# Recurrence of an encoder layer: the chunk inverse by products over 128 partitions, with full transposes of Z

## The chip, the cores and the metric

The kernel runs on one core of a Trainium2 chip. The metric is the device time of one execution in microseconds (us), the median of several runs; lower is better. The layer is computed for 2048 + 512 tokens (one stream of 2560 rows).

## The reference

One encoder layer: a combined projection, two mixers side by side (grouped attention, and RWKV-7 read in both directions), then a routed expert network with 16 experts. The changed part is the RWKV-7 recurrence:

```python
def wkv7_scan(r, decay, k, v, kk_neg, kk_b, reverse):
    def step(state, inp):
        r_t, w_t, k_t, v_t, an_t, b_t = inp
        sa = jnp.einsum('bhij,bhj->bhi', state, an_t)
        state = (state * w_t[:, :, None, :] + sa[..., None] * b_t[:, :, None, :]
                 + v_t[..., None] * k_t[:, :, None, :])
        return state, jnp.einsum('bhij,bhj->bhi', state, r_t)
```

It has 8 heads of 64 channels, each with a state of 64x64, and runs once forward and once backward. The kernel doesn't step token by token: it takes 64 tokens (a chunk) at a time. Inside a chunk the dependence of each token on those before it is a triangular 64x64 system per head, and the kernel inverts its matrix.

## The kernel before, in words

The program is a chain of stages, each a block of five instruction streams: attention inputs, attention, the inputs of the recurrence (`rwkv_inputs`), the recurrence (`recurrence`, L1194), output projection and routing, choice of tokens, experts. A stage starts when the one before it has ended.

**Layout.** Channels lie on partitions, two heads to a tile of 128 partitions (partitions 0 to 63 and 64 to 127, `halves`); four pairs (`RT` = 4, index `j`) make the 8 heads. The two directions are `g` = 0 and 1 and are independent; each has its own tiles and its own PSUM banks (`pX`, `pP`, `pZ`, `pS`). There are `NCH` = 40 chunks; direction 1 walks them backwards. A turn is the work on one chunk in both directions, half of it on chunk n (the state enters, the output leaves) and half on chunk n+1 (its inverse is prepared).

**Products.** All are plain fp32 matmuls of 64 contracted rows by 64 columns, one for each head (`heads`, L1470 to L1475). With `cross` set, the result of head h goes to the partitions of the other half. The PE program is unrolled over all 40 chunks; the programs of the other engines loop.

**The inverse.** `x3` gives the matrix, `x4` its transpose. Both are masked and get the identity (`begin`, L1404 to L1412), in `zy`: Z (index 0) and Y (index 1), kept side by side as each other's transposes. Five levels follow (`LEVELS` 2, 4, 8, 16, 32), which double the size of the inverted blocks. In each level PE makes `between` (Z's columns by `br`, 8 products for each direction), DVE masks the result into `pm` (L1417), PE makes `grown_z` and `grown_y` (8 products each, no `grown_z` in the last level), and DVE adds them into Z (L1428) and Y (L1431). The masks make that update `between`'s result times Z for one and its mirror for the other.

**The rest of a turn.** `x1`, `x2` are products with operands loaded from HBM; `through` brings the state in, `solved` applies the inverse, `state` forms the new state, `out` the output, `values` and `turned` are transposes by an identity of 64x64. ACT copies their results from PSUM to SBUF (`zs`, `uu`, `kr`, `tv`, `tbk`, `yo`), DVE updates the state (L1435, L1438), POOL masks `kr` (L1304).

**What sets the order.** It is written out by hand, engine by engine, with semaphores. In PE's stream nearly every step of a level shares its stretch with another step that uses the other pair of array tiles: `begin` alternates `x1` with `through` and `x3` with `x4`, `keys` alternates `x2` with `solved` and the first `between`, `state_and_between`, `values_and_between`, `out_and_between` and `turned_and_between` do what their names say, and `grown` alternates `grown_z` (crossed) with `grown_y` (not crossed). SP loads the next operands (bd, 512 KB, and bv, 128 KB, for each direction) when `out` of a chunk is done.

**Start of the stage.** POOL builds the masks (`full`, `beside`, `upon`, `ident`), DVE clears `st` and `pm`; PE waits for both.

Of the kernel before, what the change touches and what calls it, by code (L numbers as in the profile page):

```python
# [16 lines left out]
P = 128  # L17
# [1176 lines left out]
def recurrence(nc, ops, vals, WC, yT, w_out, WO_hi, WO_lo):  # L1194
# [6 lines left out]
    with ExitStack() as ctx:  # L1201
# [10 lines left out]
        br, kr, tbk, zy = [two(n, [P, RT, 2, C]) for n in "br kr tbk zy".split()]  # L1212
        tv, st, y_out = [two(n, [P, RT, C]) for n in "tv st yo".split()]
        one = lambda n: [sb(f"d_{n}{g}", [P, RT, C]) for g in range(2)]
        zs, uu, tmp = [one(n) for n in "zs uu tmp".split()]
        pm = [one(f"pm{l}") for l in range(NL)]
        pX, pP, pZ, pS = [[ps(f"d_p{n}{g}") for g in range(2)] for n in "XPZS"]
        s = sems("d_m d_mk d_dm d_ld00 d_ld01 d_ld10 d_ld11 d_x1 d_x3 d_x2 d_x2c d_bk d_bkc d_v d_vc d_br d_mask d_in d_init"
                 " d_x4 d_P d_Pe d_Z d_Y d_ZYe d_zs d_zsc d_u d_uc d_sn d_tmp d_S d_yo d_ye d_yst00 d_yst01 d_yst10 d_yst11 d_z d_seen d_wo d_wohi d_wolo")
# [3 lines left out]
        upper = lambda m: m[:, RT * C:].rearrange("p (j t) -> p j t", j=RT)  # L1223
# [37 lines left out]
        def _(pool):  # L1261
            k = 0
# [60 lines left out]
        def _(act):  # L1323
# [4 lines left out]
            def through(n, g):  # L1328
                act.wait_ge(s["d_zs"], 2 * n + g + 1)
                act.activation(zs[g][:], slim(pS[g]), ACT.Copy).then_inc(s["d_zsc"], 1)  # L1330

            def solved(n, g):
                act.wait_ge(s["d_u"], 2 * n + g + 1)
                act.activation(uu[g][:], slim(pS[g]), ACT.Copy).then_inc(s["d_uc"], 1)

# [4 lines left out]
            def values(m, par, g):  # L1340
                act.wait_ge(s["d_v"], 2 * m + g + 1)
                act.activation(tv[par][g][:], slim(pX[g]), ACT.Copy).then_inc(s["d_vc"], 1)
# [11 lines left out]

            def turn(n, par, i, more):
                for g in range(2):
                    through(n, g)
                for g in range(2):
                    solved(n, g)
                    if more:  # L1360
                        keys(n + 1, 1 - par, g)
                for g in range(2):
                    if more:
                        values(n + 1, 1 - par, g)
                for g in range(2):
                    out(n, par, i, g)
                for g in range(2):
                    if more:
                        turned(n + 1, 1 - par, g)

            for g in range(2):
                keys(0, 0, g)
            for g in range(2):
                values(0, 0, g)
            for g in range(2):
                turned(0, 0, g)
            with act.Fori(0, NCH // 2 - 1) as i:
# [8 lines left out]
        def _(dve):  # L1386
            for g in range(2):
                dve.memset(st[0][g][:], 0.0)
                for l in range(NL):
                    dve.memset(pm[l][g][:], 0.0)  # L1390
# [1116 lines left out]
```

## Time and profile before

| what | value |
|---|---|
| median of 3 runs | 5393.27 us (5392.49 to 5397.53) |
| the profiled execution, its own time | 5393.33 us |
| its span (first to last instruction) | 5391.5 us |
| mean granted TensorE clock over the span | 0.928 |
| busy: PE / weight loads / DVE / ACT / POOL | 81% / 74% / 58% / 39% / 20% |
| the recurrence, from PE's first to its last matmul | about 2052 to 3212 us |

The page's slices of the span (40 slices, 135 us each) show the recurrence as a stretch of its own, slices 16 to 24: PE at 6 to 7 tenths, DVE at 4 to 5, ACT at 1 to 2. In the views, one fp32 matmul leaves two MATMUL and two LDWEIGHTS records (it is made in two passes), a transpose by the array leaves one of each. The shape `64*64 64x32` is: 64 contracted rows, 64 columns of weights, a result of 64 partitions by 32 columns. "issue" as a releaser is idle time in which the engine waited for no other engine that the profile shows.

### The profile page before, as it was taken

To read this page: it belongs to the slowest core of one execution; us is meant where nothing else is said; L and a number is where in the kernel's file an instruction comes from. 1 tells how busy PE (TensorE), PEld (TensorE's weight loads), DVE (VectorE), ACT (ScalarE), POOL (GpSimd) and SP (SyncE) were. 2 spreads that over 40 slices of the span, in tenths; PEclk is the share of its full clock that TensorE was granted. 3 is DMA by queue.
4 is the path that set the end of the run, shared out by engine and by line. 5 is a ranking of instruction groups with operands and counts; after the bars stand their busy time and mean duration, and the time that the engine had idled before them with its cause. 6 is when DMAs were issued, how large, how long until landed. Compare 5 with 4: busy or idle time off the path is not lost. (4 is left out here: it accounts for less than half of the span.)

```text
span 5391.5 us, 144326 instructions
## 1 busy us (share of the span) xinstructions
PE 4389.7 (81%) x61318; PEld 3987.2 (74%) x61318; DVE 3113.5 (58%) x6054; ACT 2088.0 (39%) x4040; POOL 1069.9 (20%) x829
## 2 busy tenths in 40 slices
PE   5878888886688876777777768871399999999998
PEld 5756666664687875766767766651399999999998
DVE  6867777775688883444444445556644444444443
ACT  3347777774455551111111112220143343434433
POOL 4432222222133342110001212210101011010100
PEclk9989999999899998998999889995599999999999
DMA  7810000000433322122121124430255555555553
GB/s 159 157 46 13 16 13 14 15 12 24 154 122 134 132 102 97 52 62 60 53 62 56 57 70 142 152 112 0 67 161 170 164 163 166 162 168 167 166 162 105
DMA packets 496719, 526.60 MB, mean 98 GB/s; under 512 B 74224, under 2 KB 434672, under 8 KB 496240
## 3 DMA queue, kind: packets, MB, share of 16 engines
q1 hardware_dynamic: 390256, 413.95, 24.0%
q10 hardware_dynamic: 92480, 62.93, 5.0%
q0 software_dynamic: 13504, 42.30, 3.5%
q8 instruction: 427, 7.00, 0.5%
q14 instruction: 52, 0.43, 0.0%
HBM read 372.12 MB, written 146.99 MB: 96 GB/s over the span
## 5 line engine op out<-in xcount | busy, mean ns | idle before, releaser
L2339 DVE TENSOR_TENSOR g_wlo<-g_raw,g_whi 128x2048 fp32r<-128x2048 f32 x192 | 439.1, 2287 | 129.8 <-ACT g_whi L2301 129.8
L615 PE MATMUL sapS<-KT,saq 128*128 128x512 f32 x1024 | 369.2, 443 | 122.9 <-ACT saprob L515 115.0
L2301 ACT ACTIVATE g_whi<-g_raw 128x2048 fp32r<-128x2048 f32 x192 | 366.0, 1906 | 245.4 <-DMA g_raw<-expert_w_gate 245.4
L568 DVE TENSOR_REDUCE samx<-sapS 128x1 f32<-128x512 f32 x512 | 352.8, 689 | 184.4 <-PE sapS L615 179.1
L2406 PE MATMUL g_pD<-g_whi,g_hh 128*128 128x256 f32 (+1 forms) x1536 | 437.9, 285 | 0.6
L2406 PE MATMUL g_pD<-g_whi,g_hl 128*128 128x256 f32 (+1 forms) x1536 | 429.3, 279 | 0.0
L2406 PE MATMUL g_pD<-g_wlo,g_hh 128*128 128x256 f32 (+1 forms) x1536 | 429.0, 279 | 0.0
L523 ACT ACTIVATE saph<-sapT 128x512 fp32r<-128x512 f32 x512 | 305.7, 598 | 226.4 <-PE sapT L630 219.7
L505 POOL TENSOR_SCALAR saprob<-saprob,sarden 128x2048 f32<-128x2048 f32 x128 | 254.5, 1988 | 655.4 <-DVE sarden L587 655.4
L1116 PE MATMUL c_pP<-c_xh,c_whi 128*128 128x258 f32 x1120 | 335.4, 299 | 46.5 <-DMA c_gup<-g_lora_up 27.9
L515 ACT ACTIVATE saprob<-sapS,sanm 128x512 f32<-128x512 f32 x512 | 345.9, 686 | 9.7 <-DVE sanm L574 9.6
L1474 PE MATMUL d_pP<-d_zy,d_pm 64*64 64x32 f32 x6400 | 286.6, 232 | 57.6 <-issue 57.2
L1474 PE MATMUL d_pP<-d_zy,d_br 64*64 64x32 f32 x6400 | 287.4, 228 | 54.0 <-issue 53.7
L579 DVE TENSOR_TENSOR sapl<-sapT,saph 128x512 fp32r<-128x512 f32 x512 | 326.8, 680 | 5.7 <-ACT saph L523 5.6
L1116 PE MATMUL c_pP<-c_xh,c_wlo 128*128 128x258 f32 x1120 | 324.8, 290 | 0.0
L1116 PE MATMUL c_pP<-c_xl,c_whi 128*128 128x258 f32 x1120 | 324.4, 290 | 0.0
L1417 DVE TENSOR_TENSOR d_pm<-d_pP,d_beside 128x128 f32<-128x128 f32 x400 | 114.4, 289 | 356.3 <-PE d_pP L1474 355.9
L630 PE MATMUL sapT<-saidentf,saprob 128*128 128x128 f32 x2048 | 311.7, 275 | 9.3 <-DVE sapl L579 4.5
L2399 PE MATMUL g_pG<-g_xh,g_whi 128*128 128x320 f32 x1024 | 315.9, 309 | 0.9 <-DVE g_xl L2344 0.9
L2399 PE MATMUL g_pU<-g_xh,g_whi 128*128 128x320 f32 x1024 | 315.9, 308 | 0.0
L2399 PE MATMUL g_pU<-g_xl,g_whi 128*128 128x320 f32 x1024 | 315.8, 308 | 0.0
L2399 PE MATMUL g_pG<-g_xh,g_wlo 128*128 128x320 f32 x1024 | 315.8, 308 | 0.0
(386 smaller groups left out, 13887.0 us busy)
## 6 DMA issues: line engine op xcount, KB each, us to landing
g_raw<-expert_w_gate SPq DMA_DIRECT2D x64, 1024.0 KB, 5.0
g_raw<-expert_w_up SPq DMA_DIRECT2D x64, 1024.0 KB, 5.1
g_raw<-expert_w_down SPq DMA_DIRECT2D x64, 1024.0 KB, 5.0
ops<-c_ops SPq DMA_DIRECT2D x40, 1024.0 KB, 4.0
d_bd<-ops SPq DMA_DIRECT2D x80, 512.0 KB, 4.0
c_xh<-xT_hi SPq DMA_DIRECT2D x10, 1032.0 KB, 5.6
c_xl<-xT_lo SPq DMA_DIRECT2D x10, 1032.0 KB, 8.4
x_in<-x SPq DMA_DIRECT2D x20, 512.0 KB, 7.9
```

The lines of the kernel that those rows point to most:

```text
L515: act.activation(prob[:, h % 4, k * 512:(k + 1) * 512], pS[k][:], ACT.Exp, bias=nm[:, h % 2:h % 2 + 1], scale=SCALE, accum_out=den[:, h % ...
L523: act.activation(ph[:, h // 2 % 2, 4 * k:4 * k + 4, h % 2, :], pT[(nb * h + k) % 2][:].rearrange("p (c t) -> p c t", c=4), ACT.Copy).then_ ...
L568: ins = dve.tensor_reduce(mx[:, h % 2, k:k + 1], pS[k][:], AX.X, ALU.max)
L579: dve.tensor_tensor(pl[:, h // 2 % 2, 4 * k:4 * k + 4, h % 2, :], pT[(nb * h + k) % 2][:].rearrange("p (c t) -> p c t", c=4), ph[:, h // 2 ...
L615: mm = pe.matmul(pS[k][:], q[:, h // GH, h % GH, :], KT[:, 2 * (h // GH) + p, key0 + k * 512:key0 + (k + 1) * 512], start=(p == 0), stop=( ...
L630: mm = pe.transpose(pT[(nb * h + k) % 2][:, c * P:(c + 1) * P], prob[:, h % 4, m * P:(m + 1) * P], identf[:])
L1116: mm = pe.matmul(pP[g % 3][:, 0:TB + 2], w[:, c, m * P:(m + 1) * P], x[:, i % 2, c, :], start=(c == 0 and a == 0), stop=(c == DC - 1 and a ...
L1474: mm = pe.matmul(out(halves[1 - h if cross else h]), l(halves[h]), r(halves[h]), start=first, stop=last)
L2301: act.activation(w_hi[:, Q % NBUF, :, :], raw[:, Q % NRAW, :, :], ACT.Copy).then_inc(s["g_hi"], 1)
L2339: dve.tensor_tensor(w_lo[:, Q % NBUF, :, :], raw[:, Q % NRAW, :, :], w_hi[:, Q % NBUF, :, :].bitcast(F32), ALU.subtract).then_inc(s["g_lo" ...
L2399: mm = pe.matmul(out[:, 0:CAP], w[:, b, d, k * P:(k + 1) * P], x[:, e % 2, d, :], start=(d == 0 and i == 0), stop=(d == DC - 1 and i == 2))
L2406: mm = pe.matmul(pD[k][0:n, 0:WB], x[:, d, k * P:k * P + n], w[:, b, d, :], start=(d == 0 and i == 0), stop=(d == DC - 1 and i == 2))
```

## The change

- Only Z is kept (`zc`); `x4`, `grown_y`, `pZ` and DVE's updates of Y go. In each level PE turns Z by two transposes of 128x128 for each direction (`turned_z`, L1595), each of which turns the 64 columns of two pairs for both heads; ACT copies the result to `yq` (in the end to `yf`).
- `between`, `grown`, `through` and `solved` become products over all 128 partitions, with 64 weight columns and 64 or 128 result columns: one serves both heads of a pair. Their moving operands are block-diagonal: ACT writes each head's part into its own columns of a tile whose other part stays zero (`zb` in `blocks`, `tvb` in `values`, `stb` in `state`, `zsb` in `through`), two instructions of 64 partitions each. Two pairs alternate between the halves of the result's partitions.
- DVE's mask of a level (L1483) writes 256 columns in place of 128, by a mask `pmask`, which DVE makes at the start of the stage with 40 copies.
- PE's stream is no longer interleaved: each step stands by itself, for g = 0 and then g = 1. POOL makes an identity of 128x128 (`eye`) before the masks. SP's stream, the loads and the stores are unchanged.

```diff
-        br, kr, tbk, zy = [two(n, [P, RT, 2, C]) for n in "br kr tbk zy".split()]
-        tv, st, y_out = [two(n, [P, RT, C]) for n in "tv st yo".split()]
+        br, kr, tbk, tvb, stb = [two(n, [P, RT, 2, C]) for n in "br kr tbk tvb stb".split()]
+        st, y_out = [two(n, [P, RT, C]) for n in "st yo".split()]
+        yf = two("yf", [P, RT // 2, 2, C])
...
+            identity(nc, pool, eye[:], s["d_eye"])
...
             def through(n, g):
                 act.wait_ge(s["d_zs"], 2 * n + g + 1)
-                act.activation(zs[g][:], slim(pS[g]), ACT.Copy).then_inc(s["d_zsc"], 1)
+                for q, rows in enumerate(halves):
+                    last = act.activation(zsb[g][rows, :, q, :, :].rearrange("p a h t -> p a (h t)"),
+                                          pS[g][rows, 0:RT * C].rearrange("p (a n) -> p a n", a=RT // 2), ACT.Copy)
+                last.then_inc(s["d_zsc"], 1)
...
+            def blocks(m, l, g):
+
+                if l == 0:
+                    act.wait_ge(s["d_init"], 2 * m + g + 1)
+                else:
+                    act.wait_ge(s["d_Ze"], 2 * (NL * m + l - 1) + g + 1)
+                for h, rows in enumerate(halves):
+                    last = act.activation(packed4(zb[g][rows, :, h, :], l), cols4(zc[g][rows, :, :], l, g), ACT.Copy)
+                last.then_inc(s["d_zb"], 1)
+
+            def turned_z(m, par, l, g):
+                act.wait_ge(s["d_T"], 2 * ((NL + 1) * m + l) + g + 1)
+                y = yq[g] if l < NL else yf[par][g]
+                act.activation(y[:].rearrange("p a h t -> p (a h t)"), pT[g][:, 0:RT * C], ACT.Copy).then_inc(s["d_Te"], 1)
...
+            def level(m, l):
+                for g in range(2):
+                    blocks(m, l, g)
+                for g in range(2):
+                    turned_z(m, None, l, g)
...
-                dve.tensor_tensor(cols4(pm[l][g][:], l, g), packed4(slim(pP[g])[:, :, 0:C // 2], l), bc(mask, [P, RT] + list(mask.shape[2:])), ALU.mult)\
-                   .then_inc(s["d_Pe"], 1)
...
+                dve.tensor_tensor(flat(pmq[g][:]), bc(pP[g][:, 0:P].rearrange("p (a o t) -> p a o t", a=RT // 2, o=1), [P, RT // 2, 2, C]),
+                                  bc(flat(pmask[:, g, l:l + 1, :, :, :]), [P, RT // 2, 2, C]), ALU.mult).then_inc(s["d_Pe"], 1)
...
-                part = cols4(zy[par][g][:, :, 1, :], l, 1 - g)
-                dve.tensor_tensor(part, part, packed4(upper(pP[g])[:, :, 0:C // 2], l), ALU.add).then_inc(s["d_ZYe"], 1)
+                dve.wait_ge(s["d_Z"], 2 * (NL * m + l) + g + 1)
+                part = cols4(zc[g][:], l, g)
+                dve.tensor_tensor(part, part, packed4(grow(pP[g]), l), ALU.add).then_inc(s["d_Ze"], 1)
...
+            def turned_z(m, l, g):
...
+                for a in range(RT // 2):
+                    mm = pe.transpose(pT[g][:, a * P:(a + 1) * P], zc[g][:, 2 * a:2 * a + 2, :].rearrange("p j t -> p (j t)"), eye[:])
+                mm.then_inc(s["d_T"], 1)
+
+            def between(m, par, l, g):
+                pe.wait_ge(s["d_zb"], 2 * (NL * m + l) + g + 1)
+                for j in range(RT):
+                    mm = pe.matmul(pP[g][halves[j % 2], j // 2 * C:(j // 2 + 1) * C], br[par][g][:, j, 0, :], zb[g][:, j, :, :].rearrange("p h t -> p (h t)"),
+                                   start=True, stop=True)
+                mm.then_inc(s["d_P"], 1)
+
+            def grown(m, l, g):
+                pe.wait_ge(s["d_Pe"], 2 * (NL * m + l) + g + 1)
+                pe.wait_ge(s["d_Te"], 2 * ((NL + 1) * m + l) + g + 1)
+                for a in range(RT // 2):
+                    for h, rows in enumerate(halves):
+                        mm = pe.matmul(pP[g][rows, RT * C + a * C:RT * C + (a + 1) * C], yq[g][:, a, h, :], pmq[g][:, a, :, h, :], start=True, stop=True)
+                mm.then_inc(s["d_Z"], 1)
```

The steps of PE's new turn, each for both directions: `turned_z` (the last of chunk n), `through`, `x1` and `x3`, `solved`, `x2`, level 0 with `state` between its `between` and its `grown`, `values`, level 1, `turned`, level 2, `out`, level 3, level 4. A level is `turned_z`, `between`, `grown`.

**Level 3 and what is around it, in PE's stream.** d_pP, d_pZ, d_pX, d_pS are PSUM banks, d_zy is Z and Y, d_pm the masked result of `between`, d_pT the turned Z. Before, the last rows of `out_and_between` (level 3's `between` beside it) and the first of `grown` of level 3; the pair of rows with which the piece ends stands four times for each direction:

```order
L1474 MATMUL d_pS<-d_kr,d_tv 64x64 x2
L1474 MATMUL d_pP<-d_zy,d_br 64x32 x2
L1474 MATMUL d_pS<-d_bd,d_st 64x64 x2
L1474 MATMUL d_pP<-d_zy,d_br 64x32 x2
L1474 MATMUL d_pS<-d_br,d_uu 64x64 x2
L1474 MATMUL d_pP<-d_zy,d_br 64x32 x2
L1474 MATMUL d_pS<-d_kr,d_tv 64x64 x2
L1474 MATMUL d_pP<-d_zy,d_br 64x32 x2
L1474 MATMUL d_pZ<-d_pm,d_zy 64x32 x2
L1474 MATMUL d_pP<-d_zy,d_pm 64x32 x2
L1474 MATMUL d_pZ<-d_pm,d_zy 64x32 x2
L1474 MATMUL d_pP<-d_zy,d_pm 64x32 x2
```

In the changed kernel, the end of `out`, levels 3 and 4 and the first step of the next turn, for both directions:

```order
L1535 MATMUL d_pS<-d_kr,d_tvb 64x64 x2
L1595 MATMUL d_pT<-d_eye,d_zc 128x128 x4
L1601 MATMUL d_pP<-d_zb,d_br 64x64 x8
L1610 MATMUL d_pP<-d_pmq,d_yq 64x64 x8
L1595 MATMUL d_pT<-d_eye,d_zc 128x128 x4
L1601 MATMUL d_pP<-d_zb,d_br 64x64 x8
L1610 MATMUL d_pP<-d_pmq,d_yq 64x64 x8
L1595 MATMUL d_pT<-d_eye,d_zc 128x128 x4
L1622 MATMUL d_pS<-d_stb,d_bd 64x128
L1623 MATMUL d_pS<-d_tvb,d_kr 64x128
```

The alternation is gone, and a level is 4 transposes and 16 products where it was 48 products.

**One level in DVE's stream.** Before, level 1 of the first chunk:

```order
L1417 TENSOR_TENSOR d_pm<-d_pP,d_beside 128x32x4 x2
L1428 TENSOR_TENSOR d_zy<-d_zy,d_pZ 128x4x8x4
L1431 TENSOR_TENSOR d_zy<-d_zy,d_pP 128x4x8x4
L1428 TENSOR_TENSOR d_zy<-d_zy,d_pZ 128x4x8x4
L1431 TENSOR_TENSOR d_zy<-d_zy,d_pP 128x4x8x4
```

and now:

```order
L1483 TENSOR_TENSOR d_pmq<-d_pP,d_pmask 128x256 x2
L1493 TENSOR_TENSOR d_zc<-d_zc,d_pP 128x32x4 x2
```

Two of six instructions went, and the masks are twice as long.

## Rows read from the trace of the kernel before

**Rows 1.** Stretches: busy us (count) of PE, weight loads, DVE, ACT, POOL; PE clock; DMA.
```profile
1000.00:1500.00 500.00, 380.86 (x2513) 310.24 (x2511) 345.05 (x719) 298.96 (x684) 121.73 (x95) 0.94 0.18 56
2052.00:3212.00 1160.00, 876.89 (x37120) 823.11 (x37120) 518.05 (x1600) 215.76 (x480) 132.03 (x97) 0.90 0.19 56
```
**Rows 2.** Waits of PE from 2052 to 3212 us: us in total, times, longest.
```profile
PE d_pP L1474 <- issue: 116.5, 92, 3.6
PE d_pX L1474 <- issue: 51.4, 33, 3.3
PE d_pS L1474 <- issue: 49.5, 57, 2.3
PE d_pZ L1474 <- issue: 30.2, 35, 1.8
...
PE d_pZ L1474 <- DVE d_pm L1417: 18.7, 36, 1.5
```
**Rows 3.** DMA queues from 2052 to 3212 us: packets, MB, share of 16 engines.
```profile
q8 instruction: 292, 4.78, 1.7%
```
**Rows 4.** Short stretches inside two turns, columns as in the first group.
```profile
2111.05:2114.50 3.45, 2.81 (x128) 2.57 (x128) 1.71 (x7) 0.98 (x2) 2.65 (x2) 1.00 0.02 5
2114.50:2117.95 3.45, 2.49 (x128) 2.27 (x128) 1.92 (x7) 0.00 (x0) 0.00 (x0) 1.00 0.02 7
...
2098.00:2100.50 2.50, 2.47 (x128) 2.42 (x128) 0.78 (x3) 0.60 (x1) 0.00 (x0) 1.00 1.06 313
2100.50:2103.60 3.10, 0.10 (x6) 0.00 (x0) 0.29 (x1) 0.60 (x1) 0.00 (x0) 1.00 0.33 106
```
**Rows 5.** A stretch of `grown` at full clock, columns as in the first group.
```profile
2202.93:2203.86 0.93, 0.93 (x68) 0.92 (x64) 0.51 (x3) 0.38 (x1) 0.00 (x0) 1.00 0.06 18
```
**Rows 6.** PE in order of time, `out` alone: start us, us, line, tiles, count.
```profile
2094.70 0.28 PE L1474 MATMUL d_pS<-d_bd,d_st 64*64 64x64 f32 x4
2094.82 0.28 PE L1474 MATMUL d_pS<-d_br,d_uu 64*64 64x64 f32 x4
```
**Rows 7.** PE in order of time, first `x1` of the stage, half clock.
```profile
2052.16 1.76 PE L1474 MATMUL d_pX<-d_bd 64*64 64x128 f32 x14 [27.20 <-POOL d_upon L1297]
...
2053.68 0.45 PE L1474 MATMUL d_pX<-d_bd 64*64 64x128 f32 x2
```
**Rows 8.** PE in order of time, attention, from 128*128 to 128*64 and back.
```profile
572.73 0.28 PE L647 MATMUL sapO<-saph,VS 128*128 128x256 f32 x1
572.85 0.28 PE L647 MATMUL sapO<-sapl,VS 128*128 128x256 f32 x1
573.06 0.65 PE L674 MATMUL sapO<-sao_sb,safold 128*64 128x256 f32 x2
573.63 0.66 PE L630 MATMUL sapT<-saidentf,saprob 128*128 128x128 f32 x4
574.04 0.47 PE L615 MATMUL sapS<-KT,saq 128*128 128x512 f32 x1
```
**Rows 9.** Groups of DVE, recurrence: count, busy us, mean ns, idle before.
```profile
L1417 DVE TENSOR_TENSOR d_pm<-d_pP,d_beside 128x128 f32<-128x128 f32 x400 | 114.4, 289 | 356.3 <-PE d_pP L1474 355.9
...
L1428 DVE TENSOR_TENSOR d_zy<-d_zy,d_pZ 128x128 f32<-128x128 f32 x320 | 92.0, 287 | 114.7 <-PE d_pZ L1474 107.7
...
L1410 DVE TENSOR_TENSOR d_zy<-d_pZ,d_beside 128x256 f32<-128x256 f32 x80 | 33.2, 415 | 0.0
```
**Rows 10.** Groups of ACT, recurrence, columns as in the group before.
```profile
L1330 ACT ACTIVATE d_zs<-d_pS 128x256 f32<-128x256 f32 x80 | 30.7, 383 | 188.2 <-PE d_pS L1474 188.2
```
**Rows 11.** DVE in order of time, levels 0 and 1 of the first chunk.
```profile
2060.14 0.29 DVE L1428 TENSOR_TENSOR d_zy<-d_zy,d_pZ 128x128 f32<-128x128 f32 x1 [0.17 <-PE d_pZ L1474]
...
2062.58 0.29 DVE L1428 TENSOR_TENSOR d_zy<-d_zy,d_pZ 128x128 f32<-128x128 f32 x1 [0.24 <-PE d_pZ L1474]
```
**Rows 12.** ACT in order of time, two back to back, the stage before.
```profile
1415.02 0.84 ACT L863 ACTIVATE c_sg<-c_pX,c_dirp 128x256 f32<-128x256 f32 x2
```
**Rows 13.** POOL in order of time, one of its first masks.
```profile
2029.26 0.29 POOL L1270 TENSOR_SCALAR_AFFINE_SELECT d_full<-d_full 128x128 f32<-128x128 f32 x1
```
**Rows 14.** Groups of DVE, choice of tokens, a small operation.
```profile
L2124 DVE TENSOR_TENSOR f_ge<-f_pC,f_cap 128x32 f32<-128x32 f32 x30 | 5.8, 192 | 21.8 <-PE f_pC L2184 21.8
```

More of the change, by code:

```diff
@@ L1401, in _ @@
             dve.wait_ge(s["d_dm"], 1)
+            for q, rows in enumerate(halves):
+                for g in range(2):
+                    for l in range(NL):
+                        for h in range(2):
+                            last = dve.tensor_copy(packed(pmask[rows, g, l, q, h, :], l), cols(beside[rows, g, l + 1, :], l, g))
+            last.then_inc(s["d_z"], 1)
+            dve.wait_ge(s["d_z"], 3)
             def begin(m, par):
@@ L1466, in _, with heads @@
         def _(pe):
-            pe.wait_ge(s["d_z"], 1)
+            pe.wait_ge(s["d_z"], 2)
+            pe.wait_ge(s["d_eye"], 2)
             pe.wait_ge(s["d_dm"], 1)
-            def heads(cross, out, l, r, first=True, last=True):
-                for h in range(2):
-                    mm = pe.matmul(out(halves[1 - h if cross else h]), l(halves[h]), r(halves[h]), start=first, stop=last)
+            def heads(out, l, r, first=True, last=True):
+                for h in halves:
+                    mm = pe.matmul(out(h), l(h), r(h), start=first, stop=last)
                 return mm
@@ new lines, in turn @@
+                for g in range(2):
+                    state(n, 1 - par, g)
+                if more:
+                    for g in range(2):
+                        grown(m, 0, g)
+                    for g in range(2):
+                        values(m, par, g)
+                    for g in range(2):
+                        turned_z(m, 1, g)
+                    for g in range(2):
+                        between(m, par, 1, g)
+                    for g in range(2):
+                        grown(m, 1, g)
+                    for g in range(2):
+                        turned(m, par, g)
+                    for g in range(2):
+                        turned_z(m, 2, g)
+                    for g in range(2):
+                        between(m, par, 2, g)
+                    for g in range(2):
+                        grown(m, 2, g)
@@ new lines, in turn @@
+                for g in range(2):
+                    out(n, 1 - par, g)
+                if more:
+                    for l in range(3, NL):
+                        for g in range(2):
+                            turned_z(m, l, g)
+                        for g in range(2):
+                            between(m, par, l, g)
+                        for g in range(2):
+                            grown(m, l, g)
+            for g in range(2):
+                x1(0, 0, 0, g)
+                x3(0, 0, g)
@@ L1731 @@
+                if l == 2:
+                    for g in range(2):
+                        turned(0, 0, g)
+            for n in range(NCH):
+                turn(n, n < NCH - 1)
 NE = 16
```

385 lines of the change are left out of this document (150 added, 235 removed).

## The prediction

> **What bounds the kernel now.** First the stretches of the span: the recurrence lasts 1160 us [rows 1], 40 turns of 29.0 us, and it is the only stage that the change touches. PE is busy in 877 of them, DVE in 518, ACT in 216, so the waits of PE come next. They say "issue", 247.6 us in the four groups together, against 18.7 us for the largest wait for another engine [rows 2]. Issue is no engine's work; the third view, the DMA queues, tells what it is: 292 instruction packets, 4.78 MB, so 16 KB each and one every 4.0 us [rows 3]. The fourth view is two stretches cut at PE's pauses: exactly 128 MATMUL records with their 128 weight loads in 3.45 us, twice running, though they take only 2.5 to 2.8 us of it [rows 4]. 37120 records are 290 times 128. **PE runs at the speed at which its program comes in**, one packet of 128 records in 3.45 us at best. Once a turn it is worse: the loads of the next operands run at 313 GB/s, PE uses up its 128 records in 2.5 us and then stands for 3.1 us [rows 4]. A turn has 464 products, 928 records, 7.25 packets: 7.25 x 3.45 = 25.0 us, some 2 us for the delayed one, and 2 us for waits on other engines and uneven packets make 29.0. The Trainium skill says otherwise (Runtime: NRT & Kernel Launch, Instruction fetch mechanics): crossing a 16 KiB boundary costs one tail bump, mostly hidden. By that rule fewer instructions would buy nothing here; the rows show the stall, and they decide.
>
> **What the change takes away: packets.** A turn has now 12 pairs of transposes, one record each (24); `through` 16, `solved` 8, `between` 40, `grown` 40, `x1`, `x2`, `x3` 16 each, `state` 32, `values` 16, `turned` 32, `out` 48 products, two records each (560). 584 records are 4.6 packets, 15.7 us at 3.45. So fetching stops being the bound, and up to 29.0 - 15.7 = 13.3 us a turn come free, if nothing else takes their place.
>
> **What it gives back: array time.** The old order kept four tiles of 64x64 busy: 64 records in 0.93 us, 14.5 ns each [rows 5]. Two tiles alone give 4 records in 0.12 us, 29 ns each [rows 6]. With 128 result columns two tiles take 14 records in 1.52 us at half clock, so 54 ns at full clock [rows 7]. Four transposes of 128x128 take 0.41 us, 103 ns each [rows 8]. The new order no longer alternates, so:
> - `x3`, `values`, `turned`, `state`, `out`: 288 records on two tiles x 29 ns = 8.4 us.
> - `x1`, `x2`: 64 x 54 ns = 3.5 us.
> - transposes: 24 x 103 ns = 2.5 us.
> - `between`, `grown`: 160 records. Nothing before the change runs two column halves of the array with all 128 rows. If they overlap as four 64x64 tiles do (where two tiles share rows too [rows 5]), a record costs 29 ns, 4.6 us; if not, 58 ns (one tile's time, 2 x 29), 9.3 us. I take the first, since tiles that share rows already overlap here.
> - `through`, `solved`: 48 records with 128 columns, 54 or 108 ns, 2.6 or 5.2 us; the first again.
>
> Sum 21.6 us (28.9 at the other ends). Before, 928 records at about 15 to 20 ns were 14 to 18 us of it, under the cover of the packets. The change saves 37% of the records and adds about a fifth to a third of array time, since each is now half as well packed.
>
> **Changes of shape.** In attention the start-to-start time is 0.12 us between equal products; from 128\*128 to 128\*64 it is 0.21, 0.09 more; and the two 128\*64 records of 256 columns last 0.57 until the first transpose, where two alone would last 0.43 (each twice the 108 ns that one tile needs for 128 columns [rows 7]), 0.14 more [rows 8]. I take 0.095 us for a change of shape at full clock, near the first. The old stream had none, all its products are 64\*64. The new one has 20 a turn: 1.9 us. Bounds: 0 where PE waits anyway, 0.2 us each where a weight load is exposed too. The Trainium skill has the rule (TensorEngine Tiling (Array Packing), Key Properties): a change of tiling mode, not of tile, drains the engine. The trace agrees, with 0.09 to 0.10 us.
>
> **Clock.** 21.6 + 1.9 = 23.5 us at full clock. The recurrence runs at 0.90 now, the stage with a PE busy at 76% like it at 0.94 [rows 1]. The 3 us pauses go; I take 0.95: 24.7 us.
>
> **Waits that stay open.** A level is now a chain: DVE's sum, ACT's two copies (`blocks`), `between`, DVE's mask, `grown`, DVE's sum. A 256-column copy takes ACT 383 ns [rows 10] and two back to back 0.84 us for 0.47 each, so 0.10 us of it overlaps [rows 12]; a 128-column one is then about 0.28 and two 0.46. The mask goes from 289 to 415 ns, the sum is 287 [rows 9]. PE's part is 8 records of 29 ns and the 0.22 us of the last, twice, 0.9. With some 0.05 for each of six hand-overs that is 2.4 us, beside PE's own work for both directions of 0.4 + 0.9 + 0.2 = 1.5. So 0.9 us lies open in a level with nothing between, 4.5 in five; `state` covers half of one, and `values`, `turned` and `out` next to nothing, as ACT's `blocks` stand behind its copies of what came before. Before, a level of the first chunk took 2.44 us [rows 11] but other products ran beside it. With 0.6 for `solved` and `state`, which wait for ACT's copies, that makes 4.5 - 0.45 + 0.6, 4.7 us. ACT rises from 12 instructions a turn (5.4 us) to 52 (about 18 us of rows), still under the turn; behind its `out`, level 4's `blocks` queue, 0.9 us with the store's issue. DVE loses eight 287 ns sums and two 415 ns masks of the start and gains 1.3 us on the level masks: from 13.0 to 10.6 us. POOL's `kr` mask, the loads and stores stay where they are; the delayed packet of a turn now falls where 128 records last over 5 us and is costed at nothing (2 us a turn if that cover goes).
>
> **Sum.** 24.7 + 4.7 = 29.4 us a turn against 29.0: 40 x 0.4 = +16 us. Once: POOL's identity, two instructions of at most 0.29 us [rows 13], +0.5, as PE waits 27.2 us for POOL there [rows 7]; DVE's 40 copies of 64x32 after POOL's last, priced by a 128x32 operation of 192 ns [rows 14], 0.13 with overlap: +5 us (2 to 8). The memsets lie under POOL's 27 us. Exposed weight loads at the head of the transposes, 0.05 x 6 a turn, +12 us. Together +34 us on the profiled execution's 5393.3 us (its span 5391.5 and 1.8 around it; the median is 5393.27): **5427 us**.
>
> **Rivals.**
> - **Faster: the waits hide.** For it: PE's queue takes weight loads early, the clock may hold 1.0 without the pauses, and DVE and ACT have room. Then a turn is 23.5 + 3.2 = 26.7: 40 x -2.3 + 6 = -86, 5307 us. Anything under 28.6 us a turn is faster. Against: the chain of a level is longer than PE's work in it by rows. 0.22.
> - **No change:** the same sums ending within 10.8 us. 0.11.
> - **Column halves don't overlap.** A turn is 28.9 + 1.9 = 30.8 us at full clock, 32.4 at 0.95, and the longer products cover 1.5 us of the waits: 35.6. 40 x 6.6 + 6 = +270: 5663 us. It decides from the first level; the price is bounded by rows 5 and 6. 0.12.
> - **The clock stays low.** If transposes and thin products leave 0.85, 23.5 becomes 27.6, a turn 32.3: 40 x 3.3 + 6 = +138, 5531 us. Attention has many transposes and a clock of 0.94 or more, which speaks against. The Trainium skill has the ground for it (TensorE: Matmul & The Clock Gate, Part 4): transposes don't count as work that raises the clock. 0.10.
> - **Forecast**, 5405 to 5500: 0.45.
>
> That the change doesn't do what it says can't be here: PE's stream of the changed program shows the 4 transposes and 16 products of a level.
>
> **Numbers.** A measurement here can tell 0.2%, 10.8 us, from no change. Faster 0.22, same 0.11, slower 0.45 + 0.12 + 0.10 = 0.67. The range leaves out the column case (0.12) and the better part of the faster one (0.08): 5330 to 5560. The likeliest case alone has 5405 to 5500.
>
> **What would show it.** Right: PE's issue waits of 247.6 us fall under 40; instruction packets of the stage from 292 to about 185; records of `between` and `grown` alternate between column halves 29 ns apart; new waits of PE on DVE's mask and ACT's `zb`, near 190 us in all (40 x 4.7); PE busier than 877 us per 1160. Wrong: records of `between` 58 ns apart (column case), a clock under 0.88, PE idle in fewer than 2 us a turn (faster), or issue waits that remain, which would mean that the packets weren't the bound.

## The result, and the profile after

| | before | after |
|---|---|---|
| median, us | 5392.88 (4 runs, 5380.17 to 5397.53) | 5557.72 (4 runs, 5554.22 to 5562.02) |
| ratio | | 1.031, interval 1.0291 to 1.0329 |
| span of the profiled execution, us | 5391.5 | 5552.3 |
| recurrence, PE's first to last matmul, us | 1156.4 | 1317.1 |
| instruction packets over the whole span | 427 | 321 |

The kernel became 165 us slower where 34 were forecast. The recurrence took it all: 160.7 us longer, as is the span (160.8). A turn went from 28.9 to 32.9 us in the mean of the stage.

The stretch of the recurrence in the kernel after, columns as in [rows 1]:

```profile
2052.00:3371.50 1319.50, 1143.78 (x23360) 980.65 (x23360) 445.03 (x1240) 739.60 (x2076) 128.44 (x102) 0.95 0.17 48
```

23360 records for 37120, the clock at 0.95 for 0.90, ACT at 740 us for 216. PE's waits from 2052 to 3400 us, after:

```profile
PE d_pP L1601 <- ACT d_zb L1353: 74.6, 162, 1.3
PE d_pP L1610 <- DVE d_pmq L1483: 47.4, 117, 0.7
PE d_pX L1535 <- ACT d_tvb L1374: 41.2, 39, 1.3
PE d_pX L1535 <- POOL d_upon L1304: 28.7, 1, 28.7
```

And its instruction queue in the stage:

```profile
q8 instruction: 186, 3.05, 0.9%
```

Issue waits, 247.6 us in [rows 2], have no row any more, and the 292 packets of [rows 3] are 186. In their place PE waits for other engines: the copies into `zb`, the mask, the copies into `tvb`. The groups of ACT and DVE in the stage, after, columns as in [rows 9]:

```profile
L1353 ACT ACTIVATE d_zb<-d_zc 64x128 f32<-64x128 f32 x800 | 247.6, 309 | 160.3 <-DVE d_zc L1493 148.8
L1359 ACT ACTIVATE d_yq<-d_pT 128x256 f32<-128x256 f32 x400 | 132.0, 381 | 120.3 <-PE d_pT L1595 117.2
L1364 ACT ACTIVATE d_stb<-d_st 64x256 f32<-64x256 f32 x156 | 64.7, 415 | 2.8
L1374 ACT ACTIVATE d_tvb<-d_pX 64x256 f32<-64x256 f32 x160 | 60.4, 378 | 4.3 <-PE d_pX L1535 1.5
...
L1483 DVE TENSOR_TENSOR d_pmq<-d_pP,d_pmask 128x256 f32<-128x256 f32 x400 | 158.7, 421 | 547.1 <-PE d_pP L1601 547.0
```

A copy with half the partitions and half the columns of that in [rows 10] takes 309 ns, hardly less than its 383 (it reads SBUF and not PSUM). The state copies have next to no idle time before them (2.8 us): ACT does them as part of a queue that is full. Level 1 into level 2 of one turn, ACT and PE in order of time:

```profile
2158.76 0.66 ACT L1359 ACTIVATE d_yq<-d_pT 128x256 f32<-128x256 f32 x2
...
2159.45 1.71 ACT L1364 ACTIVATE d_stb<-d_st 64x256 f32<-64x256 f32 x4
...
2160.16 0.78 PE L1610 MATMUL d_pP<-d_pmq,d_yq 128*64 128x64 f32 x16 [0.63 <-DVE d_pmq L1483]
...
2161.18 1.56 ACT L1374 ACTIVATE d_tvb<-d_pX 64x256 f32<-64x256 f32 x4
2162.00 2.89 PE L1535 MATMUL d_pX<-d_id,d_bd 64*64 64x64 f32 x64 [1.05 <-ACT d_tvb L1374]
2162.76 1.28 ACT L1353 ACTIVATE d_zb<-d_zc 64x128 f32<-64x128 f32 x4
```

ACT runs through five groups without a gap, the four shown and copies into `zb` right before them. `turned` (L1535 at 2162.00) stands 1.05 us behind `tvb`, which stands behind state copies that nobody needs before the next turn. And `turned` then takes 2.89 us for 64 records, where 32 of them take 1.15 elsewhere. The same place as stretches, columns as in [rows 1], tells why:

```profile
2161.00:2163.00 2.00, 1.00 (x34) 1.00 (x36) 0.32 (x2) 1.90 (x6) 0.00 (x0) 1.00 0.00 0
2163.00:2166.40 3.40, 3.40 (x52) 2.95 (x50) 0.00 (x0) 1.81 (x7) 0.00 (x0) 0.50 0.02 5
2166.40:2170.00 3.60, 3.30 (x103) 3.08 (x101) 1.33 (x4) 2.16 (x6) 0.00 (x0) 1.00 0.00 0
```

Behind the two pauses (0.63 and 1.05 us) the granted clock falls from 1.00 to 0.50, that is from 2.4 to 1.2 GHz, for 3.4 us. The stage has 27 such falls after its start, and 122 us of it lie at half clock. 19 of them last 3.4 us; the other eight last 6.8 us, one in each of the last eight turns, and begin elsewhere, behind the pause of 0.62 us for `zb` in level 4. PE's longer pauses are nearly the same in every turn (0.78, 0.63, 1.05 and 0.62 us), and yet 14 turns have no fall; what decides which pause is followed by one, no run here shows. What a fall costs is shown: turns without one last 31.6 us, turns with one of 3.4 us 33.1, turns with one of 6.8 us 34.1, so 1.5 or 2.5 us.

So three theories, for the 3.2 us that a turn lasts beyond the forecast: **ACT's queue** (copies dearer than costed, and in the wrong order), **the clock** that falls behind the pauses, and **PE's own stream** (`grown`, changes of shape).

### The profile page after: what moved, and what is told of

Read it like the earlier page. It is cut to its first block and busy times, and to the rows that moved or that the text cites. A ratio compares the mean times of both kernels' runs of the same rounds, so it can differ in the third digit from the quotient of the medians.

```text
span 5552.3 us, 119126 instructions
## 1 busy us (share of the span) xinstructions
PE 4658.5 (84%) x47558; PEld 4146.2 (75%) x47558; DVE 3043.8 (55%) x5697; ACT 2611.3 (47%) x5636; POOL 1067.8 (19%) x831
## 5 line engine op out<-in xcount | busy, mean ns | idle before, releaser
L1483 DVE TENSOR_TENSOR d_pmq<-d_pP,d_pmask 128x256 f32<-128x256 f32 x400 | 158.7, 421 | 547.1 <-PE d_pP L1601 547.0
L1311 POOL TENSOR_TENSOR d_kr<-d_kr,d_upon 128x512 f32<-128x512 f32 x80 | 99.8, 1266 | 1160.7 <-ACT d_kr L1369 1160.7
L1353 ACT ACTIVATE d_zb<-d_zc 64x128 f32<-64x128 f32 x800 | 247.6, 309 | 160.3 <-DVE d_zc L1493 148.8
```

## The experiments

All but two start from the kernel after. Ratios are against the kernel before, run on the same chip.

**1. State copies later.** In ACT's `turn`:

```diff
-                for g in range(2):
-                    state(n, par, g)
                 for g in range(2):
                     values(m, other, g)
                 level(m, 2)
...
                 level(m, 3)
+                for g in range(2):
+                    state(n, par, g)
                 for g in range(2):
                     out(n, par, i, g)
```

> The changed kernel with one thing moved: ScalarE's four copies of the new state (64x256, 1.7 us a turn in its trace), which only the next turn's `through` reads, go from in front of its copies for `values` to behind its copies for level 3, where TensorE is in `out`. ScalarE's queue theory: in the trace of the changed kernel `turned` waits for `tvb` (41 us in all) and level 2's `between` for `zb` behind it, since state, values and blocks run back to back on ScalarE; then about 1.2 us a turn goes, some -48 us, 5510 (5495 to 5530), and the wait for `tvb` falls under 15 us. Rival, the turn is set by TensorE's own stream and the hand-overs of the levels: the wait only moves, 5545 to 5560.

Measured: 5602.49 us, 1.0382 (1.0365 to 1.04), slower by 45 us. The wait for `tvb` went, but `zb` took its place, in waits of up to 2.7 us:

```profile
PE d_pP L1601 <- ACT d_zb L1353: 137.1, 123, 2.7
```

In each turn the state copies and the two copies and store issues of `out` now stand in front of level 4's `blocks`. In this kernel's stretches the clock then falls for longer, 6.8 us:

```profile
2134.00:2141.10 7.10, 5.68 (x136) 4.78 (x136) 1.67 (x6) 4.26 (x12) 0.00 (x0) 1.00 0.53 173
2141.10:2147.90 6.80, 5.30 (x52) 4.26 (x53) 1.42 (x4) 2.72 (x9) 0.00 (x0) 0.50 0.21 56
```

266 us of the stage are at half clock, against 122. Nearly every turn now has a fall of 6.8 us and lasts 34.1 us, which is just what the last eight turns of the kernel after take with such a fall. So the 1.05 us that went came back as a longer wait for `zb` (2.5 us in most turns, where it was 0.62), and the slowdown of 45 us is that the clock falls in every turn. Both the expectation and its rival failed: the wait moved, and neither had a price for the clock.

**2. `grown`'s operand in one run.**

```diff
-  ... yq[g][:, a, h, :], pmq[g][:, a, :, h, :] ...
+  ... yq[g][:, a, h, :], pmq[g][:, a, h, :, :].rearrange("p q t -> p (q t)") ...
```

with the mask in the same layout, stored for both pairs.

> The changed kernel with the masked product laid out so that the moving operand of `grown` is 64 elements in a row in place of two runs of 32; its mask is stored twice for that, which adds a memset and three copies once (5 to 10 us). In the trace of the changed kernel records of `grown` are 41.5 ns apart, those of `between` 29.1 ns. If the two runs of 32 cost the 12.4 ns: 80 records a turn, 1.0 us, -40 us and +8 once, 5526 (5515 to 5540), and `grown` at 29 ns. Rival, the pace of `grown` is something else (its operands' arrival, the short step of 8 products): 41 ns stay, 5558 to 5570.

Measured: 5571.26 us (5555.45 to 5591.61), 1.0324 (1.029 to 1.0357), and records of `grown` still 41 ns apart. The rival holds: it isn't the operand's layout. Turns at full clock last 31.6 us as before; that the kernel is slower and its runs spread goes with the clock (181 us at half clock in the profiled run, against 122). Where PE does not wait inside the step (experiment 10) the same 16 records take 0.69 us for 0.78 here. The difference is at the step's middle, where the second direction begins: its first record comes about 0.05 us late and the pair behind it 0.05 more, so this is the wait for the second direction's mask, too short to be listed.

**3. Half of the `zb` copies left out.**

```diff
-                for h, rows in enumerate(halves):
+                for h, rows in enumerate(halves[:2 if l == 0 else 1]):
```

> The changed kernel; it leaves out the copy of the second head's rows into `zb` at levels 1 to 4, so that part of the inverse is not computed. 8 copies of 0.32 us fewer, 2.6 us of ScalarE a turn, 0.64 us of each level's chain. Theory that the level chain through ScalarE sets the turn: 0.3 to 0.6 us a level at four levels, -50 to -95 us, 5485. Rival, VectorE's mask and sum are as long: the waits move there, -20 us or less, above 5535.

Measured: 5466.69 us, 1.0129 (1.0112 to 1.0146): -91 us, as expected. A turn is 30.7 us, and only 3 us of the stage are left at half clock. The same stretch in the kernel after and in this one:

```profile
2055.00:3150.00 1095.00, 948.38 (x19511) 813.04 (x19509) 373.55 (x1038) 621.43 (x1744) 94.86 (x74) 0.96 0.17 48
```

```profile
2055.00:3150.00 1095.00, 958.02 (x20760) 827.81 (x20760) 392.74 (x1109) 546.30 (x1565) 107.03 (x84) 1.00 0.18 52
```

Against turns at full clock (31.6) the shorter chain is worth 0.96 us, 38 us in 40 turns; the stage lost 87, so the other 49 are the clock: 119 us fewer at half clock, some 0.4 us lost for each of them.

**4. Filler work inside the levels.** PE's `turn`, levels 1 to 4:

```diff
+                            if l == 1:
+                                values(m, par, g)
+                            if l == 2:
+                                turned(m, par, g)
+                        if l > 2:
+                            out(n, 1 - par, l - 3)
                         for g in range(2):
                             grown(m, l, g)
```

> The changed kernel with TensorE's order altered: in every level the work that depends on nothing in it stands between `between` and `grown`, while VectorE masks: `state` in level 0 as now, `values` in 1, `turned` in 2, `out` of the first direction in 3, of the second in 4 (ScalarE's copy of each half of `out` behind the level). Theory that PE's open waits are a matter of order: the wait of `grown` for the mask (117 times, 47 us) goes, and with it the gap in level 4, about -1.3 us a turn, -50 us, 5508 (5490 to 5530). Rival, the copies of ScalarE are what ends last: the waits for `zb` grow by what those for the mask lose, 5545 to 5575.

Measured: 5577.23 us, 1.0338 (1.0321 to 1.0355): the rival, 2 us above its range. The mask wait went, the wait for `zb` doubled:

```profile
PE d_pP L1601 <- ACT d_zb L1353: 146.2, 309, 1.6
PE d_pT L1595 <- DVE d_zc L1493: 42.3, 187, 0.2
```

Order on PE buys nothing while ACT is what ends last.

**5. to 7. GpSimd helps.** For the second head's rows of `zb` (5), for the state copies (6), for both and with the filler work of experiment 4 (7). In all three POOL's loop over the chunks is also written out. POOL's program, 7:

```diff
+            def blocks(m, l):
...
+                    pool.tensor_copy(packed4(zb[g][rows, :, 1, :], l), cols4(zc[g][rows, :, :], l, g)).then_inc(s["d_zp"], 1)
+            def state(n, par, g):
...
+                    pool.tensor_copy(stb[1 - par][g][rows, :, h, :], st[1 - par][g][rows, :, :]).then_inc(s["d_Sb"], 1)
```

> The changed kernel, complete, with the second head's rows of `zb` copied by GpSimd beside ScalarE's copy of the first (0.295 us for a 64x128 copy of its own in the trace, 0.309 on ScalarE). If ScalarE's copies and the clock that falls behind the pauses they make are the cause, it should do nearly what leaving those copies out did (5467): 5480 (5465 to 5500), a turn of 30.7 to 31.0 us and under 20 us of the stage at half clock, against 122. Rival, GpSimd's own waits and hand-overs take what ScalarE gives back: 5530 or more.

> The changed kernel, complete, with the four state copies of a turn done by GpSimd behind its `kr` masks in place of ScalarE. The wait of `turned` for `tvb` (1.05 us a turn) should go without the copies coming back in front of level 4, as they did when they were only moved: 40 x 1.05 us, and the half clock that begins in `turned` (most of the 122 us, at half a microsecond lost for one) with it: 5557 - 42 - 40 = 5475 (5460 to 5505). Rival, the same pause comes back in another level, whatever engine copies: 5530 or more.

> The changed kernel, complete, with both (second head's `zb` and the state copies on GpSimd) and TensorE's filler work between `between` and `grown` of each level. At full clock a turn is 31.6 us; less 1.0 for the `zb` copies, 1.05 for `tvb`, about 1.1 for the mask waits, 28.5 us; with no half clock the stage is 1145 us and the kernel 5385 (5355 to 5410), at or under the kernel before. If TensorE's own 24.5 us of products, transposes and changes of shape plus hand-overs set more than that, 5430 or more, and the change can't reach the kernel before by order and engines alone.

Measured: 5452.99 us, 1.0122 (1.0104 to 1.014); 5473.58 us, 1.0159 (1.0142 to 1.0176); 5376.83 us, 0.9976 (0.9965 to 0.9986). 6 and 7 are close to the sums (5475, 5385). 5 is 27 us under its sum and 12 below its range: its turns at full clock last 29.9 us where 30.7 to 31.0 were expected, although 47 us, not under 20, stay at half clock. PE's waits in 5, 6 and 7:

```profile
PE d_pP L1630 <- DVE d_pmq L1502: 60.2, 161, 0.7
PE d_pX L1554 <- ACT d_tvb L1393: 34.4, 39, 1.2
PE d_pP L1621 <- ACT d_zb L1372: 25.3, 80, 0.9
```

```profile
PE d_pP L1612 <- ACT d_zb L1366: 74.5, 162, 1.3
PE d_pP L1621 <- DVE d_pmq L1494: 53.0, 117, 0.8
```

```profile
PE d_pT L1621 <- DVE d_zc L1519: 35.6, 156, 0.2
PE d_pP L1637 <- DVE d_pmq L1509: 18.2, 43, 0.4
...
PE d_pP L1628 <- ACT d_zb L1381: 13.5, 42, 0.9
```

Each edit takes away most or all of the wait it aims at and leaves the other. The half-clock time falls to 47, 13 and 3 us. With ACT relieved, the order that cost 20 us in experiment 4 is worth having.

One reason why 5 gave more than its sum stands in ACT's own rows, here from 7:

```profile
2511.27 0.54 ACT L1381 ACTIVATE d_zb<-d_zc 64x128 f32<-64x128 f32 x2 [2.83 <-DVE d_zc L1519]
```

Two copies of the same half of the partitions take 0.54 us for 0.309 each, so they overlap by some 0.08 us. In the kernel after, where the copies change between the halves, four take 1.28 us, start 0.32 us apart and don't overlap at all. That the change of halves is the reason was not tested by itself.

**8. The kernel before, half the columns of `x1` and `x2`.** Its stream keeps every record.

```diff
+                if thin:
+                    return heads(False, at(wide(pX[g]), j, 0), op(par, g, OP_B, j), op(par, g, OP_A, j))
```

(and `x2` likewise, with OP_K)

> The kernel before; from the third chunk on it leaves out the second half of the columns of `x1` and `x2` (64 for 128 result columns), so that what depends on them is not computed: as many records, 64 of them half as long, 0.9 to 1.7 us less array time a turn. Theory that TensorE is bound by the instruction packets: nothing changes, within 8 us of the kernel before, and its issue waits grow. Rival, array time bounds it: -35 to -65 us.

Measured: 5392.74 us, 1.0009 (0.9999 to 1.0019). Nothing changed, and the issue waits grew from 247.6 to 260.3 us:

```profile
PE d_pP L1474 <- issue: 117.8, 93, 3.8
PE d_pX L1474 <- issue: 55.5, 39, 3.3
PE d_pS L1474 <- issue: 55.4, 62, 1.7
PE d_pZ L1474 <- issue: 31.6, 40, 1.6
```

The array time of these products was free in the kernel before; the count of instructions was the price. The places of the pauses say the same: of the 217 issue waits in the kernel before, 156 begin 127 or 128 records behind the one before, which is one packet.

**9. Filler in two pieces a level.** On top of 7: one piece between `between` and `grown`, one between `grown` and the next transposes.

```diff
+                    filler(n, m, par, l, 0)
                     for g in range(2):
                         grown(m, l, g)
+                    filler(n, m, par, l, 1)
```

> The previous version (all three edits, 5377) with the filler work of each level cut in two pieces, one between `between` and `grown`, one between `grown` and the next transposes: `state`, `values` and `turned` by direction, `out` by half a direction. ScalarE's copies for `values` and `turned` go one by one around its `blocks`, and VectorE's first state step goes in front of the sums of level 0. In the trace of the previous version `grown` to transposes is 0.91 us for 0.46 of products, five times a turn, and level 1's mask comes 0.45 late behind the state steps. Five gaps of 0.45 less five more changes of shape of 0.1, and the 0.4: 2.1 us of 28.3 a turn, 5293 (5280 to 5320). Rival, the hand-overs through ScalarE come late once TensorE stops waiting (a copy for `values` or `turned` now stands right before the next `zb`): 5340 to 5380.

Measured: 5354.37 us, 0.9973 (0.9963 to 0.9984), no better than 7 by the ratio: the kernel before ran at 5370.63 us beside it, and at 5390.38 beside 7, for a reason that isn't known. The stages compare better: 1138.7 us in 7 and 1110.9 here, 28 us less where 84 were expected. The time lies in the rival's range, but the wait that took part of the gain was none of those named:

```profile
PE d_pX L1570 <- DMA d_bv<-vals: 28.7, 38, 2.3
```

`x1` now waits for operands: their loads are issued when `out` is done, which the order had moved to the last microsecond of a turn.

**10. `out` first.** `out` in levels 1 and 2, `values` and `turned` in 3 and 4; ACT's order follows.

```diff
-                elif l == 1:
-                    values(m, par, q)
-                elif l == 2:
-                    turned(m, par, q)
-                else:
-                    out(n, 1 - par, l - 3, q)
+                elif l < 3:
+                    out(n, 1 - par, l - 1, q)
+                elif l == 3:
+                    values(m, par, q)
+                else:
+                    turned(m, par, q)
```

> The previous version (filler work in two pieces a level, 5354) with the two pieces of `out` of each direction moved to levels 1 and 2, and `values` and `turned` behind them to levels 3 and 4. The loads of the operands of the chunk after next are issued when `out` has read the old ones; in the trace of the previous version that is at the very end of a turn, and `x1` of the next turn waits 0.8 us a turn for them (28.7 us in all), while its best turn is 26.7 us against a median of 27.5. With `out` 7 us earlier that wait goes: -30 us, 5322 (5310 to 5335), a turn of 26.7. Rival, loads that run beside the levels delay the instruction packets or the engines' reads, as in the kernel before: new issue waits, 5340 to 5360.

Measured: **5305.99 us, 0.9846 (0.9832 to 0.9859)**, the fastest of all, 252 us below the kernel after with the same products, and 4 us below the expected range. The stage lasts 1072.3 us, 39 less than in 9, and every turn but the first 26.65, none at half clock once the start is over. One level of it on PE, in order of time:

```profile
2701.23 0.69 PE L1649 MATMUL d_pP<-d_pmq,d_yq 128*64 128x64 f32 x16
2701.85 0.33 PE L1573 MATMUL d_pS<-d_bd,d_st 64*64 64x64 f32 x4
2702.01 0.28 PE L1573 MATMUL d_pS<-d_br,d_uu 64*64 64x64 f32 x4
2702.13 0.28 PE L1573 MATMUL d_pS<-d_kr,d_tvb 64*64 64x64 f32 x4
...
2702.69 0.66 PE L1633 MATMUL d_pT<-d_eye,d_zc 128*128 128x128 f32 x4
2703.28 0.69 PE L1640 MATMUL d_pP<-d_zb,d_br 128*64 128x64 f32 x16
2703.89 0.33 PE L1573 MATMUL d_pS<-d_bd,d_st 64*64 64x64 f32 x4
```

No waits are left in this level (in a turn one of 0.3 us for `zb` stays, in level 0), so it shows the prices of the stream. `grown` starts at 2701.23 and the next step at 2701.85: 0.62 us, of which 16 records of 29 ns are 0.47, so the change of shape costs 0.15. The 24 records of `out` take 0.84, of which 0.70 are records and 0.14 the change; the four transposes 0.59, and at 0.109 from one start to the next without a change these are 0.44 and 0.15. The cost has two parts. The first record of a new shape starts 0.148 to 0.152 us behind the last of the old one, where a pair of records otherwise starts 0.052 behind the one before; and the second pair is late by another 0.05: the first four records of `out` above take 0.16 us (2701.85 to 2702.01), the next four 0.12.

This closes the account of a turn without waits. With 30 changes of shape (the filler pieces add ten to the 20 of the kernel after), 21.6 + 30 x 0.15 + 0.3 = 26.4 us, and 26.65 were measured; the prediction's 103 ns for a transpose, which are 109, and 54 to 55 ns for the wide records make up most of the rest.

**11. The kernel before, thin operand loads.**

```diff
+                    sp.dma_start(bd[par][g][:].rearrange("p a k j t -> p (a k j t)")[:, 0:C], ...
+                    sp.dma_start(bv[par][g][:, 0, :], vals[bass.ds(w, 1), :, 0, :] ...
```

> The kernel before; from the third chunk on it leaves out 15/16 of the bytes of the chunks' operand loads, so that stale operands enter the products; TensorE's stream is the same. If the 3.1 us pause once a turn comes from operand loads that hold up an instruction packet, it goes: 37120 records in packets of 128 at 3.45 us are 25.0 us a turn, with the waits 26.5 to 27.5 against 29.0, -60 to -100 us, 5310, and issue waits under 180 us. Rival, the pause has another cause (the packet itself): within 15 us of the kernel before.

Measured: 5333.69 us, 0.9899 (0.9884 to 0.9914), -55 us, just short of the range. Its waits:

```profile
PE d_pP L1480 <- issue: 94.0, 100, 1.5
PE d_pS L1480 <- issue: 64.4, 70, 1.6
PE d_pX L1480 <- issue: 39.2, 45, 1.5
PE d_pZ L1480 <- issue: 34.7, 42, 1.8
```

The pause of 3 us is gone (the longest issue wait is 1.8 us, where [rows 2] has 3.6; the kernel before has 32 of 1.9 us and more), so the operand loads did hold up a packet in most turns. But 232 us of issue waits stay, only 15 less than before, where I had expected under 180: the packets then set the pace throughout, with 128 records in 3.75 us (median) and not in the 3.45 of [rows 4]. The stage is 63 us shorter, and most of that is PE's busy time:

```profile
2052.60:3145.70 1093.10, 828.82 (x37120) 769.19 (x37120) 519.58 (x1600) 214.21 (x479) 128.07 (x96) 0.97 0.08 18
```

828.8 us for the same 37120 records, against 876.9 in [rows 1]. 76 us of the stage are at half clock, against 219 in the kernel before. So the long pauses cost the kernel before more through slower products behind them than as waiting time; the prediction had only the waiting, 2 us a turn.

**12. Order alone.** Experiment 10 without POOL's help; ACT copies each direction's state behind its `out`.

> The best version (5306) without GpSimd's help: ScalarE copies both heads' `zb` and the state again (each direction's state behind its `out`); the order of all engines stays. Tells how much of the way from 5558 to 5306 is order alone. By ScalarE's rows of the changed kernel a level with `out` and a state copy is 4 x 0.31 + 0.66 + 0.39 + 0.38 of store issue + 0.85 = 3.5 us on ScalarE, against 3.49 us of TensorE's best level, with the chain 0.3 us longer in each: if hand-overs then add 0.3 to 0.5 us a level, 28.3 to 29.3 a turn, 5390 (5370 to 5430), no better than the kernel before. Rival: pauses above 1 us return and the clock falls again, 5450 or more; or order is all that was missing, 5330 or less.

Measured: 5432.21 us, 1.0082 (1.0069 to 1.0096), 2 us above the range, a turn of 29.5 us (30.8 in the last eight, where PE also waits 1.0 us for DVE's sum; why was not taken apart). PE waits 92.1 us for `zb`, with pauses of 0.77 and 1.05 us in every turn, but the clock holds:

```profile
PE d_pP L1613 <- ACT d_zb L1353: 92.1, 170, 1.3
```

Of the 252 us from the kernel after to the best version, order gives 126 when it comes first (some 50 of it by keeping the clock up), GpSimd's copies on top of it the other 126. The split hangs on which comes first: PE's order alone, in the form of experiment 4, cost 20 us. Order alone stays slower than the kernel before, and so does each of GpSimd's two tasks alone (5 and 6).

## Why the prediction was right, and where it was wrong

The measured 5558 us lie inside the stated range (5330 to 5560), but the change was forecast as +34 us and came as +165. Nearest in time is the rival **the clock stays low** (5531), and it did not happen: it asked for a clock of 0.85, and 0.95 came. The forecast case is the one that ran, with two of its terms too small.

**The bound before: right.** Issue waits went from 247.6 us to none, packets from 292 to 186 (185 forecast), and experiments 8 and 11 show the bound and the stall once a turn directly. The rule of the Trainium skill (Runtime: NRT & Kernel Launch, Instruction fetch mechanics), that a boundary is mostly hidden, describes the kernel after, where no issue wait is listed; in the kernel before issue waits were a fifth of the stage. Two details were off: 3.45 us is a good packet, 3.8 the usual one, and the delayed packet costs more through the half clock behind it than as a wait (experiment 11).

**The array time: right in its parts.** `x3`, `values`, `turned`, `state`, `out` at 29 ns a record, `x1`, `x2`, `through`, `solved` at 54 to 55, transposes 109 for 103, and the open question settled: column halves with 128 rows overlap, 29 ns. 21.6 us stands within 0.3. The column rival (5663) is dead. Against the 14 to 18 us before, though, 21.6 is a fifth to a half more, not "a fifth to a third".

**Changes of shape: the term was undersized.** I took 20 x 0.095 us. Experiment 10 shows 0.14 to 0.15. The 0.095 is only the first of the two parts, the late first record (0.15 for 0.052 us); the second pair, late by 0.05 more, was left out. [rows 8] had both readings, 0.09 at one start and 0.14 over the whole piece, and the working took the smaller one; its "the trace agrees, with 0.09 to 0.10 us" leaves out the 0.14. 20 x 0.15 is 3.0 us, +1.1 a turn.

**Waits that stay open: the term that failed.** 4.7 us a turn were forecast. A turn at full clock is 31.6; less 21.6 and 3.0, that is 7.0. It is a remainder, but experiment 10 bears it out, where the same products and the changes of shape explain 26.4 of 26.65 us. The waits that the profile lists are fewer, 163 us or 4.1 a turn (near 190 were forecast); the other 2.9 are stalls shorter than the 0.2 us that a record lasts, like the one inside `grown`. Of the 2.3 missing, 1.05 are the wait of `turned` for `tvb`: the working charged ACT's 18 us "still under the turn" and never walked through its order, in which four state copies of 415 ns stand ahead of what PE waits for. The copies themselves were priced too low: a pair of 64x128 at 0.46 us, by scaling down a larger one and granting it 0.10 of overlap; one takes 0.309 and there is no overlap, so four take 1.28, 0.64 a pair, 0.18 more a level, some 0.9 a turn if all of it shows. The rest, some 0.4, wasn't taken apart further. The mask (421 ns for 415) and the places named, `zb` and the mask, were right: 122 us for those two, and 41 for `tvb`, which was not named.

**Exposed weight loads** were put at 12 us (0.3 a turn); they can't be told from the change of shape (the second late pair may be one), so I count them there.

**The clock: right in its mean, not in its mechanism.** 0.95 was forecast and 0.95 came, but I had it as a property of the load. It is 1.00 in most of the stage and 0.50 for 3.4 or 6.8 us behind some of the pauses, and each fall costs 1.5 or 2.5 us on top of the pause. That made 1.3 us a turn (32.9 less 31.6) for 1.2 forecast, an agreement by luck, and it more than doubled what experiment 3 was worth. The transposes don't lower the clock here: experiment 10 has the same 24 a turn with the stage at full clock. The Trainium skill (TensorE: Matmul & The Clock Gate, Part 4) says only that they don't count as work that raises it.

In sum, a turn: 29.4 and 0.3 were forecast; +1.1 for the changes of shape less that 0.3, +2.3 for the waits and +0.1 for the clock make 32.9. **The start** was small, as forecast: the stage begins 2.1 us later, and the 40 mask copies take 3.7 us, most of it beside `x1`. One sum of the working has a slip on which nothing rests: DVE's 13.0 less 3.1 plus 1.3 is 11.2 us a turn, not 10.6, and 11.1 came.

The rival **faster, the waits hide** was no fantasy but another kernel: it is what experiment 10 does (26.65 us a turn, 26.7 in that rival). The change took the fetch bound away and with it the cover under which the order of ACT and PE had cost nothing.

## What to carry to other kernels

Fewer, larger products help only if the chain of small copies that they need fits beside them: before predicting, walk through the queue of the engine that got the new work, instruction by instruction, with a price for its smallest tile and not a scaled one. When a bound falls away, the old order is no longer right: put work that depends on nothing into each hand-over, release buffers early enough for their loads, and give late-needed copies to an idle engine. Count a pause on TensorE at more than its length where the profile shows the granted clock fall behind it: here a fall of 3.4 us cost 1.5 us more and one of 6.8 us 2.5, behind pauses of 0.6 to 1.05 us. Price a change of shape over the whole step that follows it, and not by its first record.

## What was not expected of the hardware

- The clock: pauses of 0.63 and 1.05 us, 0.8 us apart, were followed by 3.4 us at half clock (PE busy 1.00 of 2.00 us ahead of it); a pause of 2.5 us a turn was followed by 6.8 us, and so was one of 0.62 us in the last eight turns of the kernel after. The length of a pause alone doesn't decide: the clock stayed at 1.00 behind pauses of 0.77 and 1.05 us in every turn of experiment 12, and in 14 turns of the kernel after with the same pauses as the others.
- TensorE's change of shape between two-tile or whole-array steps of fp32 costs 0.14 to 0.15 us: some 0.10 in front of the first record and 0.05 in front of the next pair (experiment 10).
- ScalarE needs 309 ns for 64x128 elements and 381 to 383 ns for 128x256, both f32: four times the elements for a quarter more time. Copies of 64 partitions that alternate between the two halves don't overlap (four in 1.28 us), two of the same half do (0.54 us, experiment 7).
- Operand loads at 313 GB/s delayed an instruction packet in most turns of the kernel before (32 issue waits of 1.9 to 3.6 us in 40 turns); thin loads gained 55 us (experiment 11), most of it in TensorE's busy time, with 76 us at half clock for 219; with 186 packets in place of 292 and the same loads no issue wait is listed.
